# Hybrid decoder step on one core: the last three experts' rows stay on chip and join the tokens by selection products in PSUM

## The chip, the core and the metric

One core of a Trainium2 chip runs the kernel. Its engines work beside each other, each through its own list of instructions: PE (matrix products and transposes), DVE, ACT and POOL (elementwise work), and SP, which here only issues transfers. They wait for each other by semaphores. 16 DMA engines move data between HBM and the on-chip memories, SBUF and PSUM (eight banks of 128 partitions by 512 floats, into which PE writes). The metric is the time of one execution on the device in microseconds (us); lower is better.

## The reference

One inference step of a one-layer decoder: 512 prompt tokens and 8 sample tokens, width 1024. Two groups of attention heads come first; their part of the kernel isn't touched but for two small transfers. What matters here is the expert stage and what closes the step:

```
g_idx = argmax(g_logits)                      # one of 4 expert groups
top_w, top_i = top_k(softmax(e_logits), 2)    # two of the 4 experts in it
gate = einsum('nd,edf->nef', h, w_gate)
up = einsum('nd,edf->nef', h, w_up)
act = silu(gate) * up * combine[..., None]
y = einsum('nef,efd->nd', act, w_down)        # 16 experts, hidden width 512
x = x + y
output = rms_norm(x, norm_final)
```

So each token x gets two rows, one from each of its experts, weighted and added, and is then normalised over its 1024 columns.

## The kernel before

Tokens are held in `x` as five tiles of rows (`TILES`): four of 128 and one of 8. The program of each engine is walked out of one list of steps, `PLAN`; the steps that matter are "experts" and "final" (one for each tile).

**Experts.** The 16 experts are worked on one after the other, those with most tokens given the largest blocks. `SIZES[j]` says how many rows the j-th expert in turn has: 128, 96, 64 or 32; rows beyond that go to an overflow loop (`overflow`, `more`), which runs only if there are any. For expert j, POOL gathers its token rows from HBM (`rows_in`); PE transposes them (`rows_of`), makes the gate product in bank 0 and the up product in bank 1 (`gate_or_up`); ACT takes the exponential of the gate (`exp_gate`); DVE forms silu(gate) times up in four operations (`gated`); PE turns that by transposes (`transpose_acts`), ACT copies them out (`acts_out`); PE makes the down product into banks 2 and 6 (`finish_down`); ACT and, for large blocks, DVE copy it into one of two buffers `y_rows` (`y_out`); and SP stores it in HBM as `expert_rows` (`y_dram`). A block of 64 or 32 rows is worked on as 2 or 4 column groups of PE side by side. In PE's list the order for j is gate j, turns of j-1, up j, rows of j+1, down j-1. In ACT's it is `exp_gate(j)`, `acts_out(j - 1)`, `rows_out(j + 1)`, `y_out(j - 1)`; in DVE's `gated(j)`, `rows_out(j + 1)`, `y_out(j - 1)`.

**Weights.** The weights of an expert are three chunks of 2 MB (gate, up, down). They are loaded in the order of `CHUNKS` into eight homes, so chunk n waits until chunk n-8 has been used. SP's loop issues them and, each time a down chunk's home is taken again, the store of the next expert's rows; the stores of experts 12 to 15 are issued behind the last chunk, down of 15. Semaphores `e_st0` and `e_st1` count the stores of even and odd experts that have landed; `stored(j)` is the count at which that of expert j and the earlier ones of its parity have. `y_out(j)` waits for `stored(j - 2)`, as it writes into the same buffer.

**Places.** At expert 0, DVE works out for each token and each of its two experts the row of `expert_rows` that holds its result (`place_results`, `y_slots`).

**Final.** When all stores have landed (SP waits for them, then signals `rows_stored`), POOL gathers for each tile its two sets of rows (`gathered`). For each tile DVE adds them with their weights to `x` (two operations), ACT sums the squares and forms the inverse root, DVE (tiles 0, 2, 4) or ACT and POOL (tiles 1, 3) scale by it and by the gain, and SP stores the tile.

## Time and profile before

| | us |
|---|---|
| three runs | 870.93, 874.99, 876.24 |
| median | 874.99 |
| the profiled execution | 872.16 |
| its span, first to last instruction | 870.3 |
| PE busy | 752.1 (86%) |
| DVE busy | 361.3 (42%) |
| ACT busy | 227.0 (26%) |
| POOL busy | 62.4 (7%) |

The times in the rows are microseconds from the start of the span. A matrix product of 32-bit floats appears as two rows of PE, since it takes two passes, so "x16" at a gate product of 128 rows is eight products. PEld is the load of the weights into the array, which overlaps PE. "L2213" is line 2213 of the kernel. What stands in brackets behind a row is the idle time ahead of it and what ended that.

In 40 slices of the span, PE's busy tenths, the granted clock and the DMA rate look like this:

```profile
PE   5988999999996788878778899589999999999910
PEclk9998999999997698999998999799999999999975
GB/s 308 61 177 161 329 40 194 24 227 125 62 139 274 313 2 1 2 2 1 25 1 1 25 98 279 122 379 268 248 392 406 390 405 387 407 385 406 412 189 198
```

The expert stage is in slices 26 to 38; the last two slices are the stage "final".

### The profile page before, as it was taken

Reading aid. Unit: us, or ns where it says so; the run is one execution under the profiler, and the core shown is the slowest. Engines: PE = TensorE matmul, PEld = TensorE weight load, DVE = VectorE, ACT = ScalarE, POOL = GpSimd, SP = SyncE. Lnnn points to the kernel's source line nnn. Section 1 sums busy time; section 2 is a strip of 40 time slices with the busy share of each in tenths; the row PEclk is TensorE's granted clock in tenths of the full one; section 3 lists DMA queues with packets and bytes.
Section 4 is the critical chain, followed back from the end, with each engine's and each line's share of the span. In section 5 each row is a group of like instructions: output and inputs, shape, how many; then the busy total and the mean of one; then the engine's idle time right before and its main releaser. Section 6 shows DMA issues by size and latency. Waiting matters only on the chain.

```text
span 870.3 us, 12141 instructions
## 1 busy us (share of the span) xinstructions
PE 752.1 (86%) x4621; PEld 402.5 (46%) x4621; DVE 361.3 (42%) x812; ACT 227.0 (26%) x579; POOL 62.4 (7%) x89
## 2 busy tenths in 40 slices
PE   5988999999996788878778899589999999999910
PEld 2455455446544334445434555334455645554500
DVE  5421014481212665665655663545323222322207
ACT  1211111112201445555565652101111101101104
POOL 0111000210000000010000000210000000000034
PEclk9998999999997698999998999799999999999975
DMA  8255915064149800000000027498799999999955
GB/s 308 61 177 161 329 40 194 24 227 125 62 139 274 313 2 1 2 2 1 25 1 1 25 98 279 122 379 268 248 392 406 390 405 387 407 385 406 412 189 198
DMA packets 86637, 171.10 MB, mean 197 GB/s; under 512 B 10042, under 2 KB 25626, under 8 KB 86546
## 3 DMA queue, kind: packets, MB, share of 16 engines
q1 hardware_dynamic: 77954, 154.15, 49.4%
q0 software_dynamic: 3296, 10.30, 3.4%
q10 hardware_dynamic: 5328, 5.86, 1.9%
q8 instruction: 38, 0.62, 0.3%
q14 instruction: 21, 0.17, 0.1%
HBM read 150.98 MB, written 21.39 MB: 198 GB/s over the span
## 4 chain that ended last, share of the span: by engine, by line
PE 55%; DVE 8%; ACT 6%; DMA 5%; issue 3%; SPq 2%; POOL 0%; ACTq 0%; DVEq 0%
PE bank L2213 17%; PE bank L2622 7%; PE bank L1679 6%; PE bank L2204 5%; PE bank L1614 4%; PE bank L2604 3%; PE bank L2247 3%; ACT reg L1110 3%; PE bank L1633 2%; DVE st L1271 2%; DMA expert_rows<-work 2%; SPq L1858 2%; ACT work L2476 1%; PE bank L1660 1%; PE bank L1616 1%
## 5 line engine op out<-in xcount | busy, mean ns | idle before, releaser
L2622 PE MATMUL bank<-reg 128*128 128x512 f32 (+1 forms) x384 | 168.7, 585 | 2.5 <-DVE work L1227 1.3
L2213 PE MATMUL bank<-reg,qreg 128*32 128x128 f32 (+2 forms) x864 | 131.7, 384 | 0.8 <-issue 0.8
L2622 PEld LDWEIGHTS bank<-reg 128*128 128x128 f32 x384 | 73.0, 199 | 73.3 <-issue 70.1
L2213 PEld LDWEIGHTS bank<-reg,qreg 128*32 128x32 f32 (+2 forms) x864 | 66.8, 138 | 61.2 <-issue 52.1
L1679 PE MATMUL bank<-reg 128*128 128x512 f32 (+1 forms) x160 | 82.1, 624 | 0.0
L2604 PE MATMUL bank<-cf,reg 128*128 128x128 f32 (+1 forms) x384 | 62.2, 290 | 17.3 <-DVE reg L2551 9.3
L2604 PEld LDWEIGHTS bank<-cf,reg 128*128 128x128 f32 (+1 forms) x384 | 43.9, 147 | 37.8 <-issue 30.2
L2476 ACT ACTIVATE work<-bank 128x128 f32<-128x128 f32 (+6 forms) x123 | 46.2, 417 | 50.2 <-PE bank L2604 28.1
L1633 PE MATMUL bank<-work,vreg 128*64 128x128 f32 x480 | 39.4, 296 | 12.6 <-ACT work L2476 11.8
L1271 DVE TENSOR_REDUCE st<-bank 128x1 f32<-128x128 f32 (+3 forms) x64 | 28.4, 485 | 31.2 <-PE bank L1616 31.1
L1633 PEld LDWEIGHTS bank<-work,vreg 128*64 128x64 f32 x480 | 27.3, 143 | 28.1 <-ACT work L2476 22.5
L1110 ACT ACTIVATE reg<-bank,st 128x128 f32<-128x128 f32 (+3 forms) x64 | 33.1, 522 | 26.7 <-DVE st L1271 25.9
L2040 DVE TENSOR_SCALAR work<-work 128x512 f32<-128x512 f32 (+3 forms) x16 | 5.6, 352 | 82.3 <-ACT work L1959 82.2
L2041 DVE RECIPROCAL work<-work 128x512 f32<-128x512 f32 (+3 forms) x16 | 39.2, 2453 | 0.6
L1030 POOL DMA_INDIRECT slot_tokens<-token,slots x10 | 10.3, 1026 | 360.0 <-DVE slots L1449 358.2
L2560 DVE COPY work<-bank 128x128 f32<-128x128 f32 (+4 forms) x40 | 15.4, 405 | 42.7 <-PE bank L2602 22.2
L2247 PE MATMUL bank<-reg,work 128*32 128x256 f32 (+1 forms) x224 | 29.5, 474 | 3.4 <-ACT work L1964 3.4
L1679 PEld LDWEIGHTS bank<-reg 128*128 128x128 f32 (+1 forms) x160 | 23.9, 176 | 16.2 <-issue 16.0
L1972 ACT COPY work<-bank 128x512 f32<-128x512 f32 (+1 forms) x16 | 8.9, 559 | 84.7 <-PE bank L2204 47.6
L1614 PE MATMUL bank<-vreg,qreg 64*128 64x128 f32 (+3 forms) x128 | 30.3, 549 | 0.3 <-ACT reg L1110 0.3
L2516 ACT COPY reg<-bank 128x512 f32<-128x512 f32 (+1 forms) x20 | 10.9, 547 | 72.8 <-PE bank L2622 72.8
L1953 ACT COPY qreg<-bank 128x512 f32<-128x512 f32 (+3 forms) x16 | 7.4, 465 | 84.6 <-PE bank L2260 50.1
(308 smaller groups left out, 910.2 us busy)
## 6 DMA issues: line engine op xcount, KB each, us to landing
reg<-w_gate SPq DMA_DIRECT2D x12, 2048.0 KB, 18.6
reg<-w_up SPq DMA_DIRECT2D x12, 2048.0 KB, 22.1
reg<-w_down SPq DMA_DIRECT2D x12, 2048.0 KB, 14.9
reg<-w_in SPq DMA_DIRECT2D x4, 2048.0 KB, 9.6
expert_rows<-vreg SPq DMA_DIRECT2D x10, 512.0 KB, 5.0
reg<-cache_sb_k SPq DMA_DIRECT2D x16, 256.0 KB, 2.8
reg<-cache_sb_v SPq DMA_DIRECT2D x16, 256.0 KB, 3.3
qreg<-w_up SPq DMA_DIRECT2D x2, 2048.0 KB
```

The costliest lines, as they stand in the source:

```text
L1110: nc.scalar.activation(prob_of(key, e)[:, 0:n], at(ring, key)[:, 0:n], ACT.Exp, bias=st[:, top:top + 1], accum_out=st[:, col:col + 1]).the ...
L1271: V.tensor_reduce(st[:, top:top + 1], at(ring, key)[:, 0:n], AX.X, ALU.max, negate=True).then_inc(sg["arg"], 1)
L1614: T.matmul(outs[e][:, 0:n], pairs[e][0], pairs[e][1], start=True, stop=False)
L1633: ins = T.matmul(to[64 * e:64 * e + 64, :], v, probT[:, turn_at[key] % 3, e, k * P:(k + 1) * P], start=(k == 0 and b != WIN), stop=(k == i ...
L1679: ins = T.matmul(at(ring, ("wout", i, group))[0:r, :], chunks_of(i)[:, chunk, 0:r], w_out[:, chunk, 512 * half:512 * half + 512], start=(k ...
L2041: link_loop(V.reciprocal(s_, s_), 3 * j + 2)
L2204: ins = T.matmul(out_bank[:, :], lhs[k], rhs[k], start=(k == 0), stop=(k == n - 1))
L2213: ins = T.matmul(bank[which][rows, at_:at_ + w], rowsT[b][:, k, r0:r0 + n], w_[:, k, h * w:(h + 1) * w], start=(k == 0), stop=(k == KD - 1))
L2247: ins = T.matmul(to[rows, 0:w], actsT[j % 2][:, 4 * r0 // P + k % per, q:q + n], w_[:, k, w * h:w * h + w], start=(k == 0), stop=(k == 3))
L2476: ins = nc.scalar.activation(dst, src, ACT.Copy, scale=scale)
L2604: ins = nc.tensor.transpose(dst, src, ident[0:src.shape[0], 0:src.shape[0]])
L2622: ins = nc.tensor.matmul(at("m", ("proj", n))[:, 0:w], hT[:, k, i * P:(i + 1) * P], win[:, pos % 2, k, 0:w], start=(k == 0), stop=(k == KD ...
```

## The change

The rows of the last three experts in turn (13, 14 and 15; `LATE` is 13) are no longer stored. They have 64 rows each, 192 in all, and stay in three halves of `y_rows` (`y_late`); the order of `SIZES` is dealt anew for that, with the same sixteen numbers. As a block of 64 rows, each lies as two column groups: columns 0 to 511 on partitions 0 to 63, columns 512 to 1023 on partitions 64 to 127.

They join the tokens by a product. For each tile, DVE makes a matrix of tokens by 192 late rows that holds the token's weight where that row is one of its two, else 0 (`pick_rows`); PE turns it (`turn_picks`) and DVE copies it out (`picked_out`), each half of it on both halves of the partitions. This is done during experts 4 to 9. In the final stage PE writes into two banks for each tile: x itself by a product with the identity, then on top of it three pairs of products of 64 rows, picks by late rows. ACT takes the squares and DVE scales out of PSUM.

The other rows are gathered by POOL as before, but in the step "experts": right after the last gather of token rows, once the stores of experts 0 to 12 have landed. A slot that points to a late row is turned into one to a row of zeros (11 more operations in `place_results`, two more stores of zeros at the start of the kernel). DVE adds tiles 0 and 1 between `gated(14)` and `gated(15)`, tiles 2 to 4 behind `gated(15)`. The gain of the last norm is loaded behind the gate chunk of expert 12, no longer at the end. POOL no longer scales tiles. The overflow loop keeps its own gathers and adds.

```
-SIZES = (P, P, 64, P, 32, P, 64, 96, P, 64, P, 64, 96, P, 64, 32)
+SIZES = (P, P, 64, P, P, 32, 96, P, 64, P, 32, 96, P, 64, 64, 64)
+LATE = 13
...
     def stored(j):
-        return 16 * sum(P // n for i in range(j % 2, j + 1, 2) for _, n in BLOCKS[SIZES[i]])
+        return 16 * sum(P // n for i in range(j % 2, min(j + 1, LATE), 2) for _, n in BLOCKS[SIZES[i]])
...
     # SP, step "experts"
-            waiting = list(range(NE))
+            waiting = list(range(LATE))
...
+                if CHUNKS[n] == ("gate", LATE - 1):
+                    sg.wait(sp, "x_dve", ("idx",))
+                    sg.wait(sp, "extra", 0)
+                    sg.wait(sp, "y_slots", 0)
+                    sp.dma_start(gain[:, :], a["norm_final"]...
             for j in waiting:
                 store_rows(j)
...
     # POOL, step "experts", behind the gathers of token rows
+            for b in range(2):
+                pool.wait_ge(sg[f"e_st{b}"], stored(LAST - 1 + b))
+            sg.wait(pool, "y_slots", 0)
+            for i in range(TILES):
+                if i == 2:
+                    pool.wait_ge(sg["e_up"], LATE + 2)
+                for k in range(2):
+                    nc.gpsimd.indirect_dma_start(gathered_rows(i, k), None, y_dram,
+                                                 bass.IndirectOffsetOnAxis(ap=y_slots[0:ROWS[i], i, k:k + 1], axis=0)
+                                                 ).then_inc(sg[f"gathered{i}"], 16)
...
     # ACT, y_out(j)
-                A.copy(y_rows[j % 2][:, 0:w], bank[2][:, 0:w]).then_inc(sg["e_y_a"], 1)
+                A.copy(y_late[j - LATE] if j >= LATE else y_rows[j % 2][:, 0:w], bank[2][:, 0:w]).then_inc(sg["e_y_a"], 1)
...
     # DVE, step "experts"
+            def add_rows(i):
+
+                r = ROWS[i]
+                sg.wait(dve, f"gathered{i}", i)
+                xi = x[0:r, i, :]
+                link(V.scalar_tensor_tensor(xi, gathered_rows(i, 0), weight[0:r, i, 0:1], xi, ALU.mult, ALU.add))
+                V.scalar_tensor_tensor(xi, gathered_rows(i, 1), weight[0:r, i, 1:2], xi, ALU.mult, ALU.add
+                                       ).then_inc(sg["early"], 1)
...
+                if 5 <= j < 5 + TILES:
+                    picked_out(j - 5)
+                if 4 <= j < 4 + TILES:
+                    pick_rows(j - 4)
+                if j == LAST - 1:
+                    add_rows(0)
+                    add_rows(1)
+            for i in range(2, TILES):
+                add_rows(i)
...
     # PE, step "final"
+            r, to = ROWS[i], final_banks(i)
+            if i == 0:
+                pe.wait_ge(sg["picked"], TILES)
+            if i == TILES - 1:
+                sg.wait(pe, "final", 0)
+            sg.wait(pe, "early", i)
+            for h in range(2):
+                if i == 3 and h == 0:
+                    pe.wait_ge(sg["e_y_a"], NE)
+                T.matmul(to[:, h, :], ident[0:r, 0:r], x[0:r, i, 512 * h:512 * h + 512], start=True, stop=False)
+            for q in range(3):
+                pe.wait_ge(sg["e_y_a"], LATE + q + 1)
+                for h in range(2):
+                    ins = T.matmul(to[:, h, :], late_pick(q, i)[64 * h:64 * h + 64, :], y_late[q][64 * h:64 * h + 64, :],
+                                   start=False, stop=(q == 2))
+            ins.then_inc(sg["late_full"], 1)
```

`final_banks(i)` are the pairs of banks (6, 7), (4, 5), (0, 1), (2, 3) and (6, 7) again.

**DVE, from the last two experts on.** L2040 to L2044 (before) and L2078 to L2082 (now) are the four operations of `gated`; before, the gathered rows were added only in the final stage (L2165, L2166). Before:

```order
L2040 TENSOR_SCALAR work<-work 128x256
L2041 RECIPROCAL work<-work 128x256
L2042 TENSOR_TENSOR work<-work,bank 128x256
L2044 TENSOR_TENSOR work<-work,bank 128x256
L2032 COPY qreg<-bank 128x4x32
L2087 COPY work<-bank 128x512
L2040 TENSOR_SCALAR work<-work 128x128
L2041 RECIPROCAL work<-work 128x128
L2042 TENSOR_TENSOR work<-work,bank 128x128
L2044 TENSOR_TENSOR work<-work,bank 128x128
```

Now (L2153 and L2154 are the two adds of `add_rows`):

```order
L2078 TENSOR_SCALAR work<-work 128x256
L2079 RECIPROCAL work<-work 128x256
L2080 TENSOR_TENSOR work<-work,bank 128x256
L2082 TENSOR_TENSOR work<-work,bank 128x256
L2070 COPY qreg<-bank 128x4x64
L2153 SCALAR_TENSOR_TENSOR x<-reg,weight,x 128x1024
L2154 SCALAR_TENSOR_TENSOR x<-reg,weight,x 128x1024
L2153 SCALAR_TENSOR_TENSOR x<-reg,weight,x 128x1024
L2154 SCALAR_TENSOR_TENSOR x<-reg,weight,x 128x1024
L2078 TENSOR_SCALAR work<-work 128x256
L2079 RECIPROCAL work<-work 128x256
L2080 TENSOR_TENSOR work<-work,bank 128x256
```

The adds of tiles 0 and 1 stand between the copy of expert 15's token rows and `gated(15)`.

**SP, the end of the loads.** `reg<-w_down ... x2` are the down chunks of experts 14 and 15. Before:

```order
L1823 DMA reg<-w_gate 128x8x512
L1823 DMA reg<-w_up 128x8x512
L1858 DMA expert_rows<-work 64x512 x2
L1823 DMA reg<-w_down 128x4x1024 x2
L1858 DMA expert_rows<-work 64x512 x2
L1858 DMA expert_rows<-work 32x256 x4
L1858 DMA expert_rows<-work 128x1024
L1858 DMA expert_rows<-work 64x512 x2
L1858 DMA expert_rows<-work 32x256 x4
L1887 DMA gain<-norm_final 128x1024
```

Now:

```order
L1858 DMA reg<-w_gate 128x8x512
L1858 DMA reg<-w_up 128x8x512
L1893 DMA expert_rows<-work 64x512 x2
L1893 DMA expert_rows<-work 32x256 x4
L1858 DMA reg<-w_down 128x4x1024 x2
L1893 DMA expert_rows<-work 128x1024
```

The store of expert 12 is the last one and stands where it stood, behind both down chunks; those of 13 to 15 and the gain are gone from behind it.

**PE, from the last down product on** (the overflow branch between the first two rows is left out). L2328 is a down product, L2417 the product with the identity, L2421 a late pair:

```order
L2328 MATMUL bank<-reg,work 64x512 x8
...
L2417 MATMUL bank<-x,cf 128x512 x2
L2421 MATMUL bank<-work,vreg 128x512 x2
L2421 MATMUL bank<-work,cf 128x512 x2
L2421 MATMUL bank<-work,vreg 128x512 x2
L2417 MATMUL bank<-x,cf 128x512 x2
```

Before, PE had nothing behind its last down product; now it has five tiles of eight products.

## Rows read from the trace of the kernel before

**Rows 1.** Busy time by stretch: microseconds, busy of each engine, granted clock, DMA share, GB/s

```profile
core 0: us, PE busy (x) PEld busy (x) DVE busy (x) ACT busy (x) POOL busy (x), PEclk, DMA share, GB/s
640.00:660.00 20.00, 20.00 (x142) 10.56 (x131) 4.52 (x8) 2.79 (x6) 0.91 (x1) 1.00 1.04 386
...
820.00:834.00 14.00, 10.18 (x180) 6.10 (x179) 2.45 (x5) 2.36 (x6) 0.00 (x0) 1.00 0.77 297
...
834.00:870.30 36.30, 0.00 (x0) 0.00 (x0) 18.48 (x13) 10.53 (x22) 15.97 (x12) 0.54 0.53 195
```

**Rows 2.** SP's queue in order of time: start, duration of the issues, line, transfer

```profile
638.85 4.78 SPq L1823 DMA_DIRECT2D vreg<-w_up  x1
...
655.19 7.35 SPq L1823 DMA_DIRECT2D reg<-w_up  x1
...
811.09 1.08 SPq L1823 DMA_DIRECT2D reg<-w_down  x2
...
812.27 23.47 SPq L1858 DMA_DIRECT2D expert_rows<-work  x13
```

**Rows 3.** Busy time by stretch, the end of the weight stream

```profile
826.00:828.00 2.00, 2.00 (x11) 0.59 (x7) 0.00 (x0) 0.00 (x0) 0.00 (x0) 1.00 1.04 406
...
828.00:830.00 2.00, 0.26 (x1) 0.07 (x1) 0.00 (x0) 0.00 (x0) 0.00 (x0) 1.00 0.65 252
```

**Rows 4.** Timeline, PE and ACT at the last two experts

```profile
824.34 3.65 PE L2247 MATMUL bank<-reg,work 128*64 128x512 f32 x16
...
830.79 0.58 ACT L1972 COPY work<-bank 128x512 f32<-128x512 f32 x1 [7.94 <-DMA expert_rows<-work]
...
831.63 1.93 PE L2247 MATMUL bank<-reg,work 128*32 128x256 f32 x32 [3.37 <-ACT work L1964]
```

**Rows 5.** Timeline, first gather, first add of tile 1, and its second

```profile
839.93 0.95 POOL L1940 DMA_INDIRECT reg<-expert_rows,y_slots  x1 [58.01 <-SPq L1892]
...
849.65 1.28 DVE L2165 SCALAR_TENSOR_TENSOR x<-reg,weight,x 128x1024 f32<-128x1024 f32 x1 [0.65 <-DMA reg<-expert_rows,y_slots]
...
850.97 1.28 DVE L2166 SCALAR_TENSOR_TENSOR x<-reg,weight,x 128x1024 f32<-128x1024 f32 x1
```

**Rows 6.** Timeline of DVE, early in the expert stage

```profile
605.01 0.69 DVE L2087 COPY work<-bank 128x512 f32<-128x512 f32 x1 [4.38 <-PE bank L2204]
```

**Rows 7.** Timeline, DVE's gated product of 64 rows; PE and ACT with small blocks

```profile
808.79 0.29 DVE L2040 TENSOR_SCALAR work<-work 128x256 f32<-128x256 f32 x1 [3.57 <-ACT work L1959]
...
810.90 0.42 DVE L2042 TENSOR_TENSOR work<-work,bank 128x256 f32<-128x256 f32 x1
...
822.01 0.44 PE L2219 MATMUL bank<-cf,work 128*128 128x128 f32 x2
...
822.37 1.95 PE L2213 MATMUL bank<-reg,qreg 128*32 128x128 f32 x64
...
822.48 0.37 ACT L1964 COPY work<-bank 128x256 f32<-128x256 f32 x1
```

**Rows 8.** Granted clock in PE's last pause; PE's gate and up of expert 0

```profile
836.00:838.00 2.00, 0.00 (x0) 0.00 (x0) 0.00 (x0) 0.00 (x0) 0.00 (x0) 0.71 0.62 209
...
562.15 9.60 PE L2213 MATMUL bank<-reg,qreg 128*128 128x512 f32 x16 [0.83 <-issue]
...
572.00 7.13 PE L2213 MATMUL bank<-reg,qreg 128*128 128x512 f32 x16
```

**Rows 9.** Timeline of PE in attention, score products of 64 rows, and the next

```profile
500.77 1.13 PE L1614 MATMUL bank<-qreg 64*128 64x512 f32 x4
...
501.83 0.29 PE L1616 MATMUL bank<-cb 128*128 128x128 bf16 x2
```

**Rows 10.** Timeline, the last tile behind DVE's adds, and its store

```profile
864.30 1.06 ACT L2000 ACTIVATE reg<-x 8x1024 f32<-8x1024 f32 x1 [0.80 <-DVE x L2166]
...
867.57 0.34 SPq L1897 DMA_DIRECT2D out_y_s<-x  x1
```

**Rows 11.** Stores of expert rows (L1858), all 37: issue to landing

```profile
DMA to landing us min/median/max: 1.5/9.5/18.1
```

More of the change, by code:

```diff
@@ L50 @@
 CAP = 5 * P
-POOL_FINAL = (1, 3)
 FIRST_PAIR = 4
@@ L73, in first_row @@
     return sum(BY_RANK[:turn(j)])
+LATE_ROW = first_row(LATE)
+LATE_ROWS = sum(SIZES[LATE:])
 def host_constants():
@@ L1784, in body @@
         sg.mark(f"gathered{i}", i, 32)
-        sg.mark("combined", i)
+        sg.mark("early", i)
+        sg.mark("late_full", i)
         sg.mark("ssq_final", i)
-        sg.mark("final_pool" if i in POOL_FINAL else "final", i)
+        sg.mark("final", i)
         sg.mark("st_y", i, 16)
@@ L1812, in overflow @@
                     one(v)
+            if after:
+                after()
     def load_all(sp, e, sem):
@@ L1993, in more @@
                 act.wait_ge(sg["v_down"], v + 1)
-                A.copy(y_rows[0][:, 0:512], bank[2][:, :]).then_inc(sg["v_y"], 1)
+                A.copy(y_more[:, 0:512], bank[2][:, :]).then_inc(sg["v_y"], 1)
             overflow(act, more)
@@ L2080, in y_out, with add_more @@
+            def add_more():
+                dve.wait_ge(sg["v_gathered"], 32 * TILES)
+                for i in range(TILES):
+                    r, xi = ROWS[i], x[0:ROWS[i], i, :]
+                    for k in range(2):
+                        link(V.scalar_tensor_tensor(xi, gathered_more[0:r, 2 * i + k, :], weight[0:r, i, k:k + 1], xi,
+                                                    ALU.mult, ALU.add))
+                V.memset(smi[:, 40:41], 0).then_inc(sg["v_added"], 1)
             def y_out(j):
@@ L2157, in more @@
                 dve.wait_ge(sg["v_down"], v + 1)
-                V.tensor_copy(y_rows[0][:, 512:D], bank[6][:, :]).then_inc(sg["v_y"], 1)
-            overflow(dve, more)
+                V.tensor_copy(y_more[:, 512:D], bank[6][:, :]).then_inc(sg["v_y"], 1)
+            overflow(dve, more, add_more)
         elif kind == "final":
```

175 lines of the change are left out of this document (105 added, 70 removed).

## The prediction

> **What bounds it now.** I first read the busy table by stretch. From 640 us on the 16 DMA engines are full and PE is full too (20.00 of 20 us); between 834 us and the end PE does nothing [rows 1]. So two things set the end: a stretch in which weights and products are equally tight, and a tail of 36.3 us without PE. The tail is what the change is about.
>
> Next I read SP's queue. From 638.85 us on, putting one weight chunk into the queue takes SP 5 to 7 us, where two take 1.08 us when there is room: the queue is full [rows 2]. From there the pace is that of the bytes. The last two chunks (down of experts 14 and 15) are issued from 811.09 to 812.17, and the stores of experts 12 to 15 behind them, from 812.27 on. The two-microsecond stretches show the stream at 406 GB/s until 828 and breaking off between 828 and 830 [rows 3]. PE used the last down chunk at 831.63; it was not late itself, ACT was: its copy out of down 14 stood until 830.79 for the store of expert 12 (same half of `y_rows`), and the copy that PE needed stood behind it [rows 4]. That store was issued from 812.27 on and landed up to 18 us later (the longest of all stores is 18.1 us [rows 11]), behind both weight chunks. This is the most useful row of the trace for what follows.
>
> Then the tail: the stores land, the first gather is issued at 839.93, the fourth has landed when DVE starts at 849.65, tile 1 is added up at 850.97 + 1.28 = 852.25 [rows 5], and so on through adds, squares and scales to 870.3.
>
> **The change part by part.** The sum is made on the profiled span.
>
> *Order of sizes.* The same 16 sizes are dealt out again, so PE's product time is the same in sum; only the last three become 64, 64, 64 instead of 128, 64, 32. Expert 4 now has 128 rows instead of 32, so its gate and its up take 7.1 us each instead of 1.95 [rows 7, 8], and the homes freed by what comes behind them are free up to 10 us later: up 7, issued at 655.19, may go out as late as 665. The queue is full at that point, with some 10 to 18 us of bytes in it, by the median and the longest landing of a store [rows 2, 11], so it hardly runs dry. If it held only half of that, 4 to 6 us of the stream would be lost; I take 6 as the bound.
>
> *Picks and slots.* 11 more small DVE operations after `place_results`, some 0.2 us each, 2.2 us in all: DVE stands idle for 4.38 us just behind that place [rows 6]. The pick rows, their ten turns on PE (under 2 us in all) and the 30 copies out of bank 7 are spread over experts 4 to 9, where DVE is busy for about a quarter of the time (4.5 of 20 us [rows 1]) and bytes, not PE, set the pace. Cost 0; without that cover it would be about 2 us. Two more zero stores at the start of the kernel are issued in a stretch far from any tight one: 0.
>
> *The gain load* moves from the tail into the full queue: 0.5 MB at 0.4 MB per us is 1.3 us more stream. The stores of experts 2 to 12 hold 32 rows more than before and the row gathers in that time 32 less; these cancel.
>
> *The early gathers.* They shall run "while these run". But they wait for `e_st0` and `e_st1` up to expert 12, and store 12 still stands on SP behind down 14 and down 15. By the wait of ACT [rows 4] it lands where it landed, just ahead of 830.79: 830.8 + 1.3 = 832.1 us. The weights of 14 and 15 arrive only just before. So nothing is left of the experts to hide the gathers under, except what now waits for them.
>
> *The adds on DVE.* `add_rows(0)` and `add_rows(1)` stand ahead of `gated(15)` on DVE. DVE would reach them at about 811 us and stand there. Behind it waits gated 15, for that PE's last turns and down 15, for that the late rows' last third, for that all five final tiles. In place of one wait at the end there is one in the middle of the chain:
> - store 12 landed: 832.1
> - gathers 0 to 3 issued and landed, tiles 0 and 1 added: 839.93 to 852.25 in the trace, 12.3 us [rows 5]: 844.5
> - gated 15 (64 rows): 808.79 to 810.90 + 0.42 = 811.32 for the first three operations and 0.42 for the fourth, 3.0 us [rows 7]: 847.5
> - turns and ACT's copy: 0.44 and 0.37 us [rows 7]; at half clock 1.2 us: 848.7
> - down 15: a 64-row down takes 3.65 us [rows 4]. PE has then been idle for some 20 us. The trace shows the granted clock at 0.71 in the stretch from 836 to 838, where PE had been idle since 831.63 + 1.93 = 833.6, on its way from the upper level (2.4 GHz) to the lower (1.2 GHz), and the first products after such a pause took 9.60 us against 7.13 for the same work at full clock [rows 4, 8]: 2.5 us more. 6.1 us: 854.8
>
> *The final stage on PE.* For each of five tiles (the tile of 8 rows too, as the columns that stream are 512 all the same) four full passes for x and twelve passes of 64 rows. A full pass is 7.13 / 16 = 0.45 us at most, 0.43 between starts [rows 8]: 1.7 us. For the 64-row passes the nearest row is the score product, two row groups into two banks, also 512 columns: four passes in 501.83 - 500.77 = 1.06 us instead of 4 x 0.43 = 1.72 [rows 9]. So the groups run beside each other. Three such pairs 3.2 us, a tile 4.9, five tiles 24.5: 879.3. Bounds: 0.86 a pair gives 21.5 in all, one after the other (1.72) gives 34.3. The Trainium skill (TensorEngine Tiling, Performance Considerations) states for a contraction of 64 a tiling of two, up to twice as fast; by that the stage would take 21.5 us. The trace bears out less, 1.06 and not 0.86, and I take the trace.
>
> *Behind the last tile*: square, Ln, Exp, DVE's scale and the store. In the trace from 864.30 to 870.3, 6.0 us [rows 10]: 885.3. The adds of tiles 2 to 4 (2.6 us each on DVE, from 847.5) end before PE comes to them; their gathers too.
>
> Sum: 885.3 against a span of 870.3, +15.0 us. The profiled execution took 872.16, so 887.2; it lay 2.8 us below the median of the runs shown (874.99). I say **888 us**, 1.5% slower.
>
> What was won: final's adds off the tail, some 10 us on DVE, and the gathers' start 8 us earlier. What it costs: a down product, its clock, and a final stage of 24.5 us on PE, all behind the same landing.
>
> **The rivals.**
> - *Not slower: store 12 lands early.* If the store of 128 rows, now one transfer instead of six, overtakes the weights, it could land soon after its issue at about 813; the shortest landing of such a store is 1.5 us [rows 11]. Then adds until 828, down 15 at about 832 to 836 (its weights land near 829), final stage 860.5, end 866.5: 868 us. The point from which it is no loss is a landing before about 818. Against it: the store of the same expert in the same place stood in the queue until 830.8. The Trainium skill (DMA: Bandwidth & Descriptors, Queues, rings and completion order) says that descriptors are taken in ring order, though a later one may finish first; by that an overtaking of two whole chunks is not to be had, and the landing in the trace agrees. 0.12, and in it 0.04 for faster by over 1%, if the final stage is at its lower bound too.
> - *Row groups don't overlap here*, because each pair accumulates into the banks of the one before: 15 x 0.66 = 9.9 us more, 897 us. The score rows speak against it, but they never had three pairs on one bank. 0.12.
> - *The ring runs dry after the 128-row blocks*: stream up to 6 us later, 893. 0.08.
> - *The clock stays at half through the final stage*: 24.5 us more, 912. Against it: in the trace the loss of 2.5 us is that of 5 us at half clock, after which it was full [rows 8]. 0.04.
> - *Forecast*: 0.64; its own range is 881 to 894.
>
> **How the numbers follow.** Low end: pairs at 0.86 (-3.0), no clock loss (-2.5), landing 2 us earlier, is 880; high end: the serial case and the landing 3 us later, 900. Range 879 to 900. About 1% is what a measurement of this kernel tells from no change. Slower by over 1% (above 883.7): most of the forecast and the last three rivals, 0.82. Within 1%: the low end of the forecast and most of the early landing, 0.14. Faster: 0.04.
>
> **What would show it.** The last store of expert rows lands near 832 and the first gather out of `expert_rows` is issued right behind it, not before 825. DVE's first add of x starts near 839 with over 20 us of idle time before it, and the fourth ends near 844.5. PE idle from about 828 to 848, granted clock 0.5 at the end of that gap. down 15 ends near 855. The final stage has a period of 4.9 us per tile. The forecast is wrong if gathers are issued while PE still works on expert 14, if PE has no gap ahead of down 15, or if a tile of the final stage takes over 6 us.

## The result: 1.8% slower, and the profile after

| | before | after |
|---|---|---|
| median, us | 872.96 (867.11 to 876.24) | 887.94 (885.42 to 892.28) |
| ratio, 95% interval | | 1.0184 (1.0113 to 1.0256) |
| span of the profiled execution | 870.3 | 886.1 |
| PE busy | 752.1 | 777.9 |

The forecast was 888 us, with a range of 879 to 900. How much of that was for the right reasons is the subject of the rest.

PE's busy tenths, the granted clock and the rate of the DMA engines, in 40 slices of the span of the changed kernel (its page, part 2):

```profile
PE   5988999999995889779788897799999999998457
...
PEclk9998999999996799999999999799999999999869
...
GB/s 303 72 162 181 318 70 178 48 248 108 75 136 279 250 1 2 1 1 24 1 1 24 96 130 203 264 315 228 367 397 385 392 383 386 381 390 393 309 122 97
```

Before, PE was nearly idle in the last two slices. Now the hole lies in slices 38 and 39, and PE works to the end. In slices 30 to 37 the stream runs at 381 to 397 GB/s; before it ran at 385 to 407 there. No term of the forecast had that.

Busy time by stretch of the changed kernel, with the columns of [rows 1]:

```profile
820.00:834.00 14.00, 10.14 (x58) 4.41 (x54) 0.00 (x0) 1.14 (x3) 0.00 (x0) 0.88 0.91 365
834.00:850.00 16.00, 0.00 (x0) 0.00 (x0) 7.73 (x8) 0.59 (x1) 10.48 (x10) 0.66 0.77 266
850.00:852.00 2.00, 1.28 (x4) 0.59 (x6) 1.97 (x3) 0.37 (x1) 0.00 (x0) 0.50 0.00 0
834.00:886.10 52.10, 29.88 (x98) 9.66 (x98) 21.75 (x19) 9.60 (x23) 10.48 (x10) 0.81 0.34 123
```

From 834 us on PE is busy for 29.88 of 52.10 us, where it was busy for 0.00 of 36.30 [rows 1]. The 16 us ahead of 850 hold nothing of PE, and behind them the granted clock is 0.50, the lower level (1.2 GHz).

SP's queue of the changed kernel, the last weight chunks and the last store (compare [rows 2]):

```profile
800.72 6.80 SPq L1858 DMA_DIRECT2D reg<-w_up  x1
...
815.73 1.89 SPq L1858 DMA_DIRECT2D reg<-w_down  x2
817.72 1.99 SPq L1893 DMA_DIRECT2D expert_rows<-work  x1
```

The last down chunks are issued at 815.73; before it was 811.09 [rows 2].

The chain from there, in the timeline of the changed kernel (compare [rows 4] and [rows 5]):

```profile
828.34 5.35 PE L2328 MATMUL bank<-reg,work 128*64 128x512 f32 x16 [2.53 <-issue]
...
834.63 0.59 ACT L2012 COPY work<-bank 128x512 f32<-128x512 f32 x1 [9.75 <-DMA expert_rows<-work]
834.81 0.95 POOL L1973 DMA_INDIRECT reg<-expert_rows,y_slots  x1 [52.23 <-DMA expert_rows<-work]
...
841.23 1.28 DVE L2153 SCALAR_TENSOR_TENSOR x<-reg,weight,x 128x1024 f32<-128x1024 f32 x1 [30.09 <-DMA reg<-expert_rows,y_slots]
...
844.70 1.28 DVE L2153 SCALAR_TENSOR_TENSOR x<-reg,weight,x 128x1024 f32<-128x1024 f32 x1 [0.87 <-DMA reg<-expert_rows,y_slots]
...
846.02 1.28 DVE L2154 SCALAR_TENSOR_TENSOR x<-reg,weight,x 128x1024 f32<-128x1024 f32 x1
...
847.22 0.29 DVE L2078 TENSOR_SCALAR work<-work 128x256 f32<-128x256 f32 x1
...
849.78 0.42 DVE L2082 TENSOR_TENSOR work<-work,bank 128x256 f32<-128x256 f32 x1
...
850.26 0.69 PE L2300 MATMUL bank<-cf,work 128*128 128x128 f32 x2 [16.57 <-DVE work L2082]
...
851.41 5.95 PE L2328 MATMUL bank<-reg,work 128*64 128x512 f32 x16 [0.46 <-ACT work L2004]
```

ACT's copy and POOL's first gather both wait for one thing, the last store of expert rows, and both go on at 834.6 to 834.8. DVE has then stood for 30.09 us, in front of the first add. `gated(15)` follows the fourth add with no gap (847.22), PE's turns follow `gated(15)` (850.26, after 16.57 us of idle time that ended with DVE's product), down 15 follows ACT's copy. It is the chain that was forecast, link for link.

The times above are counted from the start of the execution, and the expert stage doesn't begin at the same time in each execution. The gate chunk of expert 5, "gate 5" from here on, is issued at 622.60 us before and at 620.38 in the changed kernel. From it to the up chunk of expert 15:

```profile
622.60 0.37 SPq L1823 DMA_DIRECT2D reg<-w_gate  x1
...
796.69 7.80 SPq L1823 DMA_DIRECT2D reg<-w_up  x1
```

```profile
620.38 0.37 SPq L1858 DMA_DIRECT2D reg<-w_gate  x1
```

That is 174.1 us before (the first two rows) and, with the up chunk at 800.72, 180.3 now. The stream lost 6.2 us over this stretch, and 2.2 us of it don't show in the times from the start.

The final stage, same view: the start of tile 0, its first pair, tile 1, and the close.

```profile
857.29 1.98 PE L2417 MATMUL bank<-x,cf 128*128 128x512 f32 x4
...
859.21 1.13 PE L2421 MATMUL bank<-work,vreg 64*128 64x512 f32 x4
...
861.98 1.98 PE L2417 MATMUL bank<-x,cf 128*128 128x512 f32 x4
...
880.65 1.01 ACT L2041 ACTIVATE work<-bank 8x1024 f32<-8x1024 f32 x1 [2.81 <-PE bank L2421]
...
883.65 0.34 SPq L1931 DMA_DIRECT2D out_y_s<-x  x1
```

### The profile page after: what moved, and what is told of

Same layout as the page of the kernel before. It is cut to its first block, busy times and chain, and to the rows that moved or that the text cites. A ratio compares the mean times of both kernels' runs of the same rounds, so it can differ in the third digit from the quotient of the medians.

```text
span 886.1 us, 12369 instructions
## 1 busy us (share of the span) xinstructions
PE 777.9 (88%) x4711; PEld 411.0 (46%) x4711; DVE 375.5 (42%) x869; ACT 224.4 (25%) x577; POOL 57.0 (6%) x87
## 4 chain that ended last, share of the span: by engine, by line
PE 55%; issue 9%; DVE 7%; ACT 6%; DMA 3%; POOLq 0%; POOL 0%; ACTq 0%; DVEq 0%
PE bank L2294 15%; PE bank L2730 7%; PE bank L1685 6%; PE bank L2285 5%; PE bank L1620 4%; PE bank L2712 3%; PE bank L2328 3%; ACT reg L1116 3%; PE bank L1639 2%; DVE st L1277 2%; PE bank L2421 2%; ACT work L2584 1%; PE bank L2417 1%; PE bank L1622 1%; PE bank L1666 1%
## 5 line engine op out<-in xcount | busy, mean ns | idle before, releaser
L2294 PE MATMUL bank<-reg,qreg 128*32 128x128 f32 (+2 forms) x960 | 116.6, 363 | 3.8 <-DMA reg<-w_gate 1.9
L2294 PEld LDWEIGHTS bank<-reg,qreg 128*32 128x32 f32 (+2 forms) x960 | 63.4, 132 | 53.8 <-issue 40.6
L2285 PE MATMUL bank<-reg,work 128*128 128x512 f32 x112 | 49.5, 595 | 0.0
L2668 DVE COPY work<-bank 128x128 f32<-128x128 f32 (+4 forms) x40 | 15.5, 405 | 39.3 <-PE bank L2710 20.5
L2285 PEld LDWEIGHTS bank<-reg,work 128*128 128x128 f32 x112 | 20.7, 190 | 23.6 <-issue 23.4
L2173 DVE COPY work<-bank 128x512 f32<-128x512 f32 (+1 forms) x9 | 5.7, 632 | 59.5 <-PE bank L2285 28.1
```

Source lines behind the costliest of these rows:

```text
L2285: ins = T.matmul(out_bank[:, :], lhs[k], rhs[k], start=(k == 0), stop=(k == n - 1))
L2294: ins = T.matmul(bank[which][rows, at_:at_ + w], rowsT[b][:, k, r0:r0 + n], w_[:, k, h * w:(h + 1) * w], start=(k == 0), stop=(k == KD - 1))
```

## The experiments

The question was twofold. Is the wait of the adds for store 12, in front of `gated(15)`, what makes the kernel slow (theory A)? And why does the end of the weight stream come 4 us later than before (6 us, counted within the stage), which nothing in the forecast gave (theory B: the gain load; B2: the picks; the order of sizes; later theory S, below)? Each run's ratio is to executions of the kernel before on the same chip.

The last two columns are read from the profiled execution: the rate from 640 to 820 us, and the time from the issue of gate 5 to that of up 15, which doesn't depend on when the stage begins.

| | median, us | ratio (95%) | span | GB/s | gate 5 to up 15, us |
|---|---|---|---|---|---|
| before | 872.96 | | 870.3 | 398 | 174.1 |
| the change | 887.94 | 1.0184 (1.0113 to 1.0256) | 886.1 | 389 | 180.3 |
| adds behind `gated(15)` | 877.55 | 1.0102 (1.0044 to 1.0160) | 874.8 | 388 | 181.1 |
| store 12 ahead of the down chunks | 883.00 | 1.0153 (1.0106 to 1.0201) | 878.7 | 389 | 180.3 |
| both | 878.34 | 1.0094 (1.0063 to 1.0124) | 872.9 | 389 | 180.3 |
| before, with the new sizes | 869.66 | 0.9994 (0.9958 to 1.0031) | 868.6 | 402 | 173.5 |
| gain last | 888.47 | 1.0199 (1.0145 to 1.0254) | 885.9 | 387 | 179.9 |
| no picks | 891.56 | 1.0204 (1.0140 to 1.0268) | 892.4 | 388 | 180.7 |
| both, and x joined on DVE | 869.06 | 0.9993 (0.9955 to 1.0030) | 866.6 | 386 | 181.4 |
| before, constants 128 bytes longer | 877.09 | 1.0076 (1.0046 to 1.0107) | 875.3 | 387 | 178.7 |
| the change, constants 384 bytes longer | 881.28 | 1.0114 (1.0078 to 1.0151) | 882.8 | 401 | 175.1 |
| both, x on DVE, constants 384 bytes longer | 859.21 | 0.9881 (0.9848 to 0.9915) | 857.4 | 402 | 175.9 |
| before, SBUF shifted by 128 bytes | 874.59 | 1.0074 (1.0042 to 1.0106) | 872.4 | 389 | 178.4 |
| before, SBUF shifted by 256 bytes | 871.94 | 1.0032 (0.9999 to 1.0065) | 871.0 | 399 | 173.6 |

### The adds behind gated(15)

```
-                if j == LAST - 1:
-                    add_rows(0)
-                    add_rows(1)
-            for i in range(2, TILES):
+            for i in range(TILES):
                 add_rows(i)
```

> The changed kernel, with DVE's adds of tiles 0 and 1 moved behind the gated product of expert 15; nothing else is touched. Theory (the adds stand ahead of the last expert on DVE, and the whole last expert waits for the gathers): the gated product of 15 goes at about 826 instead of 847 us, PE's last turns soon behind; ACT's copy of them still stands behind its copy out of down 14, which waits for store 12 (834.6 in the changed kernel), so down 15 runs from 836 to 839.5 at full clock. The final stage then starts when tile 0 is added up, at 844, and takes 23.4 us and the 5.5 us behind it: span 873 to 875 instead of 886.1, some 12 us less, within 1% of the kernel before. Rival 1 (it is the 23.4 us of PE's final stage that costs, wherever the adds stand): the span stays within 3 us of 886. Rival 2 (the stream of weights is what came later): span falls by no more than 3 us.

Timeline of this run:

```profile
834.29 0.58 ACT L2012 COPY work<-bank 128x512 f32<-128x512 f32 x1 [9.88 <-DMA expert_rows<-work]
...
835.20 3.65 PE L2325 MATMUL bank<-reg,work 128*64 128x512 f32 x16 [1.69 <-ACT work L2004]
...
844.03 3.75 PE L2414 MATMUL bank<-x,cf 128*128 128x512 f32 x4 [5.18 <-DVE x L2154]
```

The store lands where it landed (834.29), but down 15 now starts 0.9 us behind it, at full speed (3.65 us), where it started 16.8 us behind it. The final stage still waits for tile 0's adds (5.18 us, `<-DVE x`), and its first products run at the lower clock (granted clock 0.50 from 842 to 848 us; 3.75 instead of 1.98 us). The span is 11.3 us shorter; 1.1 us of that is an earlier start of the stage (gate 5 at 619.26, not 620.38). Theory A holds for the place of the adds: two lines in DVE's order cost some 10 us of span. The medians differ by 10.4 us, and all four executions (875.98 to 882.87) are faster than all four of the change; by the ratios it is 0.8%, with intervals that overlap, so the size is less certain than the wait.

### Store 12 ahead of down 14

In SP's loop of loads, ahead of `load_chunk`:

```
+                if CHUNKS[n] == ("down", LAST - 1):
+                    store_rows(waiting.pop(0))
                 load_chunk(sp, n, expert_reg[CHUNKS[n][1]])
```

> The changed kernel, with the store of expert 12 issued by SP ahead of the down chunks of experts 14 and 15 instead of behind them; nothing else is touched. Theory (the gathers start when this store lands, and it lands in the order of the queue): it lands two chunks earlier, 2 x 5.2 = 10.4 us, at about 824 instead of 834.6, the first gather is issued right behind it, DVE's fourth add ends at about 837, down 15 ends at about 846 to 847, span 876. As the gathers now share the DMA engines with the last two chunks, up to 4 us of that may be lost: 876 to 880. Rival (the store was not held by the chunks but by its own write or by the engines): it lands at 832 to 835 as before and the span stays at 885 to 887.

Timeline of this run:

```profile
823.33 0.95 POOL L1975 DMA_INDIRECT reg<-expert_rows,y_slots  x1 [42.30 <-DMA expert_rows<-work]
...
833.52 1.28 DVE L2155 SCALAR_TENSOR_TENSOR x<-reg,weight,x 128x1024 f32<-128x1024 f32 x1 [23.96 <-DMA reg<-expert_rows,y_slots]
...
838.41 1.28 DVE L2155 SCALAR_TENSOR_TENSOR x<-reg,weight,x 128x1024 f32<-128x1024 f32 x1 [2.28 <-DMA reg<-expert_rows,y_slots]
...
843.97 0.69 PE L2302 MATMUL bank<-cf,work 128*128 128x128 f32 x2 [9.18 <-DVE work L2084]
```

With nothing but two weight chunks taken out of the store's way, the first gather goes out at 823.33 instead of 834.81, 11.5 us earlier (1.6 us of it, again, an earlier start of the stage). The store's landing was the position in the queue, as the forecast said. But the gathers now share the DMA engines with the weights: the first add starts 10.2 us behind the first gather instead of 6.4, and tile 1's 4.9 us later instead of 3.5. Of the 11.5 us, 6.3 are left at PE's turns (843.97 against 850.26). The span is 7.4 us shorter, but the ratios (1.0153 and 1.0184, intervals overlapping) don't show that the time is.

### Both

The edits of the two runs above together.

> The changed kernel with both edits: store of expert 12 ahead of the last two down chunks, adds of tiles 0 and 1 behind the gated product of expert 15. Theory: gathers from about 824, tiles 0 and 1 added by 837; down 15 waits only for its weights. If gathers and chunks share the engines evenly, these land at 838 to 840 and down 15 ends at 842 to 844; the final stage 23.4 us and 5.5 behind: span 871 to 873. If the chunks are hardly slowed, down 15 ends at 838 and the span is 867. In both cases within 1% of the kernel before or a little faster. Rival (PE's final stage costs, not the waits): 880 or more.

Timeline of this run:

```profile
824.17 0.96 POOL L1975 DMA_INDIRECT reg<-expert_rows,y_slots  x1 [42.11 <-DMA expert_rows<-work]
...
839.14 5.04 PE L2327 MATMUL bank<-reg,work 128*64 128x512 f32 x16 [2.98 <-DMA reg<-w_down]
...
844.11 1.98 PE L2416 MATMUL bank<-x,cf 128*128 128x512 f32 x4
```

Alone they gave 11.3 and 7.4 us of span, together 13.2: they shorten the same wait. Down 15 now waits for its weights (`<-DMA reg<-w_down`, 839.14), and the final stage starts at 844.11 instead of 857.29. But it started at 844.03 with the adds moved alone, where down 15 began at 835.20: what the earlier store wins at the gathers, the weights lose. By the ratios the two edits (1.0094) are no faster than the adds alone (1.0102); 1.9 us of one execution's span is all that speaks for the store. The kernel is still 0.9% slower than before. Down 15 starts at 839.14, against 831.63 behind ACT's copy [rows 4]; the slower stream and the gathers beside it both delay its weights, in shares that no run separates. Behind it stand five tiles of PE at 4.69 us, 23.4 us.

### The kernel before with the new sizes

```
-SIZES = (P, P, 64, P, 32, P, 64, 96, P, 64, P, 64, 96, P, 64, 32)
+SIZES = (P, P, 64, P, P, 32, 96, P, 64, P, 32, 96, P, 64, 64, 64)
```

> The kernel before with only the new order of the block sizes (128, 128, 64, 128, 128, 32, 96, 128, 64, 128, 32, 96, 128, 64, 64, 64). Theory (the stream of weights keeps its pace, the order costs nothing by itself): the store of expert 12 lands within 1 us of 830.8; the last down product is 1.7 us longer and its block's gated product and copies 1.5 us, which partly replaces the wait of 3.4 us there: span 870 to 873 against 870.3. Rival (the ring of homes runs dry after the early blocks of 128 rows, the 2.5 us by which store 12 came later than forecast are its doing): store 12 lands 2 to 6 us later and the span is 874 to 877.

No difference in time. In its timeline store 12 is down and ACT goes on at 827.21, not within 1 us of 830.8 as expected but 3.6 us earlier (1.8 us of it an earlier start of the stage), and the stream is not slower (402 against 398 GB/s):

```profile
827.21 0.59 ACT L1972 COPY work<-bank 128x512 f32<-128x512 f32 x1 [9.45 <-DMA expert_rows<-work]
```

The ring did not run dry, and the order of sizes does not explain the late stream.

### The gain last

The load of the gain moves from behind the gate chunk of expert 12 to behind the last store.

```
-                if CHUNKS[n] == ("gate", LATE - 1):
...
-                    sp.dma_start(gain[:, :], a["norm_final"]...
             for j in waiting:
                 store_rows(j)
+            sp.dma_start(gain[:, :], a["norm_final"]...
```

> The changed kernel, with the load of the last norm's gain issued behind the last store instead of behind the gate chunk of expert 12. The store of expert 12 landed at 834.6 in the changed kernel, 2.5 us later than forecast, and at 827.2 in the kernel before with the new order of sizes alone; something in the change slows the stream of weights by up to 7 us. Theory A (it is the gain load, 0.5 MB and one source row for all partitions, priced at 1.3 us): SP's issue of up 15 falls from 800.7 towards 795, the store lands at 828 to 830 and the span is 880 to 882. Theory B (the gain costs its bytes, 1.3 us, and the delay comes from elsewhere, as it is already 6 us before the gain load is issued): up 15 is issued at 799 to 800, the store lands at 833, span 884 to 886.

Timelines of this run: SP's last up chunk, and ACT's copy behind the last store.

```profile
800.41 6.87 SPq L1858 DMA_DIRECT2D reg<-w_up  x1
```

```profile
834.30 0.58 ACT L2011 COPY work<-bank 128x512 f32<-128x512 f32 x1 [9.85 <-DMA expert_rows<-work]
```

800.41 and 834.30, against 800.72 and 834.63 with the gain in the stream. Theory B falls, and the 1.3 us that the forecast charged for the gain were not seen: 0.3 us, less than such times differ between runs with the same stream (179.9 to 181.4 us in the table's last column).

### No picks

```
-                if 5 <= j < 5 + TILES:
-                    picked_out(j - 5)
-                if 4 <= j < 4 + TILES:
-                    pick_rows(j - 4)
+                if j == 5:
+                    V.memset(dead, 0.0)
+                    V.memset(vreg[:, 4096:4880], 0.0).then_inc(sg["picked"], 1)
```

PE's `turn_picks` is gone too. The late rows don't reach the tokens in this run.

> The changed kernel without the making of the picks during experts 4 to 9 (no pick rows, no turns on PE, no copies out of bank 7; the picks are zero, so the late rows don't reach the tokens; all the rest runs as it did). Theory B1 (the copies and turns in these experts slow the stream, as the delay against the kernel before with the new sizes grows from 1.7 to 6.1 us between 685 and 741 us): up 15 is issued at 795 to 796 instead of 800.7, the store of expert 12 lands at 829 to 830, span 881 to 882. Theory B2 (picks are hidden and cost nothing, the delay is the scatter of the stream between programs): up 15 at 799 to 801, store at 833 to 835, span 885 to 887.

The whole expert stage of this execution lies some 6 us later (gate 5 is issued at 626.49, not 620.38, the last down chunks at 822.21, not 815.73), for a reason ahead of that stage that stays open. Its pace is that of the change: 388 GB/s, and 180.7 us from gate 5 to up 15 against 180.3. So the picks do not slow the stream, as forecast. The time itself (891.56) can't price them, as it holds those 6 us.

### x joined on DVE instead of PE

Both edits of above, and PE's product with the identity is dropped. DVE adds PSUM to `x`, ACT squares `x`, DVE scales `x` in SBUF, one tile behind.

```
-                T.matmul(to[:, h, :], ident[0:r, 0:r], x[0:r, i, 512 * h:512 * h + 512], start=True, stop=False)
...
-                                   start=False, stop=(q == 2))
+                                   start=(q == 0), stop=(q == 2))
...
+            sg.wait(dve, "late_full", i)
+            xi = x[0:r, i, :].rearrange("p (a b) -> p a b", a=2)
+            V.tensor_tensor(xi, xi, final_banks(i), ALU.add).then_inc(sg["joined"], 1)
```

> A candidate to beat both: the two edits of e3_both (store of expert 12 ahead of the last two down chunks, adds behind the gated product of expert 15), and no identity products: PE makes only the three late pairs for each tile, DVE adds them out of PSUM to x, ACT squares x and DVE scales it in SBUF. Theory (in e3_both the end was set by five tiles of 4.69 us on PE behind down 15 at 844.1, of which 1.91 each are the identity products): PE ends at 844 + 5 x 2.78 = 858, DVE has the adds until 849.4, then 5 x 1.3 us from PSUM and 5 x 1.3 us of scaling until about 863, and 3 us behind: span 865 to 867 instead of 872.9, some 0.5% below the kernel before. Rival (something else, such as the landing of the gathers or of the last chunk, sets the end): span within 2 us of 872.9.

Timeline of this run:

```profile
840.54 6.11 PE L2330 MATMUL bank<-reg,work 128*64 128x512 f32 x16 [4.20 <-DMA reg<-w_down]
...
846.58 1.13 PE L2418 MATMUL bank<-work,vreg 64*128 64x512 f32 x4
847.54 1.02 PE L2418 MATMUL bank<-work,cf 64*128 64x512 f32 x4
...
857.08 1.03 PE L2418 MATMUL bank<-work,vreg 64*8 64x512 f32 x4
857.94 1.88 PE L2418 MATMUL bank<-work,cf 64*8 64x512 f32 x8
```

The late rows of the five tiles take PE from 846.58 to 859.8 (857.94 + 1.88), and PE no longer waits for the adds of a tile before it starts. From the second pair of tile 0 to the first of tile 4, eleven pairs with no identity product between them, it is 857.08 - 847.54 = 9.54 us, 0.87 a pair. The loss is gone, and nothing is won yet (0.9993): the stream is still at 386 GB/s.

### 128 bytes in the constants

What was left of the change was a list of column numbers in the bf16 constants that had grown from 128 to 192 columns, 128 bytes per partition. All SBUF buffers allocated behind it start 128 bytes higher, `reg0`, `reg1` and `work` at 384 past a multiple of 512 bytes instead of at 256. Six of the eight homes of the weights lie in `reg0` and `reg1`; the other two, in `vreg` and `qreg`, start beside a multiple of 256 bytes in every kernel here. Theory S: that slows the stream. The kernel before with 64 unused columns, and the change with 192 more, which puts the buffers back:

```
+        "pad": np.zeros((P, 64)),
```

```
+        "pad": np.zeros((P, 192)),
```

> The kernel before with one more constant of 64 columns of zeros (128 bytes for each partition) that nothing reads. It moves every on-chip buffer behind the constants by 128 bytes, as the change does with its longer count row: the weights' homes then start at 384 instead of 256 modulo 512. Between 640 and 820 us the stream ran at 382 to 412 GB/s (mean 398) in the kernel before, 402 with the new sizes, and at 379 to 399 (mean 389) in the changed kernel and in all five made from it, whether the gain load, the picks or the adds were moved or not. Theory S (the address shift is what slows the stream): mean 388 to 391 GB/s, SP's issue of up 15 near 800 instead of 796.7, the store of expert 12 near 834, and as both the tail and the last experts hang on it, span 873 to 876. Rival (the shift is nothing, some other traffic or work of the changed kernel slows the stream): mean 396 to 403 GB/s, span 868 to 872.

> The changed kernel with one more constant of 192 columns of zeros that nothing reads, so that the buffers are moved by 512 bytes in all and stand modulo 512 where they stood in the kernel before. Theory S: the stream runs at 398 to 402 GB/s between 640 and 820 us, up 15 is issued at 795 to 797, the store of expert 12 lands at 828 to 830 instead of 834.6, span 880 to 882. Rival: 387 to 391 GB/s, store at 833 to 835, span 885 to 887.

Busy time by stretch, the kernel before with 64 unused columns:

```profile
640.00:820.00 180.00, 180.00 (x1252) 93.84 (x1245) 51.08 (x61) 20.39 (x43) 8.21 (x9) 1.00 1.04 387
```

And the change with 192 more:

```profile
640.00:820.00 180.00, 180.00 (x1386) 95.35 (x1384) 62.65 (x107) 20.33 (x44) 8.14 (x9) 1.00 1.04 401
```

387 against 398 GB/s, and 401 against 389 (the last column). 64 columns that nobody reads make the kernel before 0.8% slower, with a span of 875.3 us where theory S expected 873 to 876; the change without its shift is 1.1% slower, not 1.8%. In its timeline the last store and the first gather are at

```profile
832.10 0.59 ACT L2013 COPY work<-bank 128x512 f32<-128x512 f32 x1 [9.64 <-DMA expert_rows<-work]
832.28 0.94 POOL L1974 DMA_INDIRECT reg<-expert_rows,y_slots  x1 [45.75 <-DMA expert_rows<-work]
```

These are the times of the forecast (832.1), but by chance: in this execution the stage began 1.7 us later than before and 3.9 later than in the change (gate 5 at 624.32). Up 15, the store and the span (799.38, 832.10, 882.8) all lie behind what was expected (795 to 797, 828 to 830, 880 to 882), mostly for that reason. Counted within the stage, up 15 is issued after 175.1 us instead of 180.3: 5.3 us are back, and 1.0 us is left against the kernel before.

### The same without the constants: 128 and 256 bytes of SBUF

The runs above also made the constant tensor in HBM longer. So the kernel before got an unused SBUF buffer only, of 128 or of 256 bytes per partition, behind the constants:

```
+    sb("shift", [P, 32])
```

```
+    sb("shift", [P, 64])
```

> The kernel before with nothing but an unused SBUF buffer of 128 bytes per partition placed behind the bf16 constants, so that every later SBUF buffer starts 128 bytes higher; the constants in HBM stay as they were (in the run with 64 unused zero columns both had moved). Theory D, the place in SBUF where the weights land sets the pace of the stream: like that run, 640 to 820 us at about 387 GB/s instead of 398, time 0.7 to 1.0% above the kernel before, 875 to 878 us. Theory H, what counted there was the larger constant tensor in HBM: pace 398 GB/s, time as before within 0.3%.

> The same with 256 bytes per partition, so that the two large weight regions start at a multiple of 256 bytes again, but no longer at 256 past a multiple of 512. If a start that is no multiple of 256 bytes is what costs (theory D256): no loss, 397 to 402 GB/s and the time of the kernel before within 0.3%. If any other place than the one of the kernel before costs, or a period of 512 bytes counts (D512): 387 to 392 GB/s and 0.5 to 1.0% above it. Theory H expects the time of the kernel before here as well.

Busy time by stretch, 128 bytes:

```profile
640.00:820.00 180.00, 179.43 (x1215) 92.71 (x1207) 49.64 (x58) 19.66 (x41) 8.23 (x9) 1.00 1.04 389
```

256 bytes:

```profile
640.00:820.00 180.00, 180.00 (x1233) 93.22 (x1221) 51.10 (x61) 20.49 (x43) 8.17 (x9) 1.00 1.04 399
```

With 128 bytes the stream is at 389 GB/s and the time up by 0.74%, as with the longer constants: theory H falls, it is the place in SBUF (D). With 256 bytes it is at 399 GB/s. Of the starts tried, 0 and 256 past a multiple of 512 bytes keep the pace and 384 past it doesn't: a period of 256 bytes, not of 512. Other offsets were not tried, and as all buffers behind the constants moved together, that it is the homes of the weights among them is argued from their share of the bytes. The time of that run, 1.0032 (0.9999 to 1.0065), doesn't exclude a small loss of another kind. One of the ten executions of the 128-byte run took 1894.88 us; the cause stays open, and the ratio leaves it out.

The Trainium skill (DMA: Bandwidth & Descriptors, How a descriptor splits into AXI transactions) has a rule that fits: a transaction begins at a 256-byte boundary, and a descriptor that doesn't start there spends beats of 32 bytes on bytes it doesn't use. The page says it of what is read; here the shifted side is the one written. An estimate from it: 4 beats more on the 64 of a 2 KB row (gate, up) and on the 128 of a 4 KB row (down), in six of eight homes, is a mean of some 4% (0.75 of the mean of 6.3, 6.3 and 3.1%); the traces show 2.3% (389 against 398) to 3.0% (389 against 401). That the unused beats are the mechanism is argued, not shown.

### The best version

Both edits, x on DVE, and 192 unused columns.

> The candidate e6_x_on_dve (span 866.6) with the same 192 columns of zeros. Theory S: everything behind the stream comes 4 to 6 us earlier, down 15 is ended at 841 instead of 846.6, span 861 to 863, some 1% below the kernel before. Rival: span 866 to 868, no difference to e6_x_on_dve.

Timeline of this run:

```profile
816.84 0.95 POOL L1977 DMA_INDIRECT reg<-expert_rows,y_slots  x1 [36.62 <-DMA expert_rows<-work]
...
831.59 5.35 PE L2331 MATMUL bank<-reg,work 128*64 128x512 f32 x16 [3.99 <-DMA reg<-w_down]
...
836.87 1.13 PE L2419 MATMUL bank<-work,vreg 64*128 64x512 f32 x4
...
854.94 0.34 SPq L1935 DMA_DIRECT2D out_y_s<-x  x1
```

1.2% faster than the kernel before (0.9881, 0.9848 to 0.9915), and faster than expected (a span of 861 to 863); 2.3 us of the span is an earlier start of the stage (gate 5 at 617.99, against 620.25 in the run without the columns). Down 15 waits only for its weights, the tail behind it is 857.4 - 836.9 = 20.5 us where it was 36.3 without PE [rows 1]. The gain is the sum of three things, each with a run to it: the adds out of `gated(15)`'s way with the store ahead of the weights (1.0184 to 1.0094), x off PE (to 0.9993), and the stream at its full pace (to 0.9881). What the store's place adds here was not tried by itself.

## Why the prediction was right, and where it was not

**The likeliest case was the one that came.** Step by step:

| step | forecast | measured |
|---|---|---|
| store 12 landed | 832.1 | 834.6 |
| gathers, tiles 0 and 1 added | 12.3 | 12.5 (834.8 to 847.3) |
| gated 15 | 3.0 | 3.0 |
| turns and copy | 1.2 | 1.2 |
| down 15 after a pause | 6.1 | 5.9 |
| five tiles | 24.5 | 23.3 (857.3 to 880.6) |
| behind the last | 6.0 | 5.5 |
| end of the span | 885.3 | 886.1 |

**The landing of store 12** was 2.5 us late, the step that missed by most. The forecast took the landing of before, 830.8, and added 1.3 us for the gain. The position in the queue was right (the run with the store ahead shows it), the gain's term was over-sized (0.3 us seen), and a term was missing: the pace of the stream. It ran at 389 instead of 398 GB/s, since the constants had grown by 128 bytes. A term for a shift of every later buffer should have stood in "the change part by part"; the constant stands in the code of the change. Taken back, it moves the ratio from 1.0184 to 1.0114, some 6 us. The miss looks smaller than it was: from gate 5 the store is down after 214.3 us (834.63 - 620.38), against 208.2 before (830.79 - 622.60), 6.1 us later and not 1.3. Of the 4.8 us that were missing, 2.2 were hidden by the earlier start of the stage in the execution that was profiled.

**Order of sizes: 0** was right; the kernel before with the new sizes is the same within 0.4%. The rival with a dry ring falls. **Picks and slots: 0** was right for the stream, by the pace without them.

**The adds on DVE** stood where forecast, and were the largest single cause: without them in front of `gated(15)` the span is 11.3 us shorter, some 10 of it theirs.

**PE's gap** was forecast from 828 to 848 and lay from 833.7 (828.34 + 5.35) to 850.3. Down 14 itself came later (828.34, not 824.34 [rows 4]), which the trace puts down to no wait; its activations were out at 824.50 + 0.38, so its weights are the likely reason. It cost nothing, as the chain went by the store. The clock at its end was 0.50, as forecast, and down 15 took 5.95 us where 6.1 were charged for that.

**A pair of 64-row products** was put at 1.06 us, from the score rows [rows 9]. Three took 2.77 us (859.21 to 861.98), 0.92 each. The row groups do run beside each other, also where a pair adds to the banks of the pair before, so the serial rival falls. The four passes for x took 1.92 us (857.29 to 859.21) where 1.7 were charged, so a tile took 4.69 us where 4.9 were: two errors of opposite sign. The score row was misread as the price of a pair, for it stands between other products; with no identity product between them a pair takes 0.87 us (the run with x on DVE), and the rest, 0.2 us of a tile's pairs and 0.2 of its four passes, comes only where the two kinds alternate. The Trainium skill gives a contraction of 64 a tiling of two, up to twice as fast (TensorEngine Tiling (Array Packing), Overview, Theoretical Speedup). The 0.87 us agrees with it: half of four full passes is 0.86, which the forecast had as its lower bound only.

**The other rivals.** The early landing did not come: a store does not overtake two chunks ahead of it. The clock did not stay at half: the first identity product of tile 0 took 1.98 us for four passes, like those of the next tiles.

**The sum hit because errors of both signs cancelled.** +2.5 for the landing and +0.2 for the gathers stand against -0.2, -1.2 and -0.5. Without the shift of the buffers the measured loss is 1.1%, and the forecast of 1.5% would have been too high by 3 to 4 us; the closeness of the 888 us is partly luck. So is the span of 886.1 in one execution: with the stage beginning where it did before, it would have been some 2 us longer.

**What stays open**: why the expert stage begins at different times (gate 5 at 617.99 to 626.49 us in the fourteen profiled executions); what the store ahead of the chunks is worth in time; and whether the unused beats are what costs at 128 bytes.

## What to carry to other kernels

Work "overlapped" with a stage is only overlapped if nothing of that stage stands behind its wait on the same engine: two adds in front of the last gated product turned a transfer's latency into a hole in PE. A small store that others wait for goes earlier when it is issued ahead of the large loads in its queue, but what it releases may then share the engines with these loads: here the gathers began 11.5 us earlier, and no fall of the time was shown. When a constant or a buffer changes its length, look where the buffers behind it now start: here the stream into large buffers was faster with a start at a multiple of 256 bytes than 128 bytes beside one. And before two executions are compared by times from their start, find one event early in the stage and count from it.

## What the runs showed of the hardware

A stream of 2 MB weight chunks into SBUF, with all 16 DMA engines full, runs at 398 to 402 GB/s when the two large target buffers start at a multiple of 256 bytes in each partition (five kernels: before, with the new sizes, with 256 bytes of shift, and the two realigned ones) and at 386 to 389 GB/s when they start 128 bytes beside one (nine kernels). From gate 5 to up 15 it is 173.5 to 175.9 us in the five and 178.4 to 181.4 in the nine, some 5 us; in the whole kernel before it was 0.7 to 0.8%.

A store issued behind two 2 MB loads on the same queue let its followers go 17 us after its issue (817.72 to 834.6); issued ahead of them, the first gather goes 11.5 us earlier, 9.9 counted from gate 5.

Gathers that run beside the weights take longer: the first add follows the first gather after 10.2 us instead of 6.4.

Products of 64 rows on two row groups, 512 columns, take 0.87 us for four passes in a run of eleven such pairs, half of what four passes of 128 rows take. Where they alternate with full products, three pairs take 2.77 us and the four full passes 1.92.
